# Gated scan: states between blocks of 128 tokens in place of two levels, blocks of 8 and pairs by one stationary tile, norm with tokens in partitions

## The chip, the cores and the metric

One core of a Trainium2 chip runs the whole program in one launch. The metric is the device time of an execution in microseconds (us). TensorE (PE; PEld is its weight load) multiplies, VectorE (DVE) and ScalarE (ACT) do the elementwise work, SyncE (SP) issues the loads.

## The reference, cut to what matters

A block (modulated norm, gated convolution, retention, MLP) is followed by a pooling mixer and a gated linear recurrence (HGRN2) with 16 heads of 128 channels over 512 tokens. The change lies in the recurrence alone:

```python
log_f = jnp.logaddexp(jnp.log(lbf), jnp.log1p(-lbf) + jax.nn.log_sigmoid(fz))
k = (1.0 - lbf) * jax.nn.sigmoid(-fz)
...
A = jnp.einsum('bhtd,bhsd,bhtsd->bhts', qc, kc, jnp.exp(diff))
o = jnp.einsum('bhts,bhsv->bhtv', A, vc) + jnp.einsum('bhtd,bhdv->bhtv', qc * jnp.exp(bc), S)
S = exp(b_last) * S + jnp.einsum('bhsd,bhsv->bhdv', kc * jnp.exp(b_last - bc), vc)
...
o = o * lax.rsqrt(jnp.mean(o * o, axis=-1, keepdims=True) + EPS)
return (o * norm_g * jax.nn.silu(gate)) @ w_out
```

So token t reads token s at or before it with the product of all forget gates f between them, channel by channel; each head's output is normed over its 128 channels and gated.

## The kernel before, in words

**Work and order.** Every large product is three TensorE matmuls in fp32r (weights and activations split in a high and a low part: `three`, L302 to L305; one such group of three over 512 tokens is called a triple here). The weights stream through SBUF in units of 128x1024: ScalarE makes the high part (L1405) and VectorE the low part (L704). In the scan, `project(h)` is three columns of eight triples for head h (forget gate, query, output gate: 24 triples, counted n = 0 to 23). The three engines run the same loop, each in its own program and its own strict order; semaphores tie them together. Between the triples, at the positions listed in `SIDE`, TensorE does one step of `mixing(h - 1)`, the attention of the head before; `norms` hands finished heads to a second side program (`turn`).

**Decay by levels.** VectorE's `prepare(h)` (n = 10 on) makes products of gates within blocks of 8 tokens around a pivot (`W`), their reciprocals (`IW`, L1262), and from them `f` and `qp`, whose product gives the scores inside each block of 8 (level 0, L586). Then the levels L = 8, 16, 32, 64, 128, 256: at each, the second half of a block of 2L tokens reads the first half. TensorE multiplies `k` by `q` (L597, L600, L604, L608); VectorE waits for that product, scales `q` and `k` in place by block totals to the next level (L1303, L1304), makes the next totals (L1309), and copies what it wants out of PSUM by mask (L1291, L1315) or ScalarE copies it (L1714 to L1726) into the score tile `A`, which covers 512x512 tokens. These products are plain f32 and each shows as two instructions.

**Output and norm.** Four matmuls with V stationary and rows of `A` moving (512, 384, 256 and 128 columns, L615) give the output with channels in partitions. ScalarE squares it, four matmuls with ones (L390) sum it over channels, VectorE gates it (L1323). Every fourth head VectorE takes the reciprocal root of all four heads' sums (`rsqrt`, L753 to L776, 13 small operations, each waiting for the one before), and for each head makes a diagonal tile (L784), TensorE spreads it by a product with ones (L412, in the next head's period), and VectorE multiplies (L1337).

Of the kernel before, what the change touches and what calls it, by code (L numbers as in the profile page):

```python
# [13 lines left out]
T = 512  # L14
# [114 lines left out]
def build(nc, a):  # L129
    with ExitStack() as ctx:  # L130
# [27 lines left out]
        PS = [ctx.enter_context(nc.psum_tensor(f"PS{i}", [128, T], F32)) for i in range(8)]  # L158
        with nc.sbuf_tensor("PSP", [128, 4, T], F32R) as PSP:
            pass  # L160
        QP0, QP1, W, IW = (sb(n, [128, T]) for n in ("QP0", "QP1", "W", "IW"))
        QP = [QP0, QP1]
# [15 lines left out]
        LVB, OB, RBK = [3, 4], 5, 6  # L178
        LEVELS = (8, 16, 32, 64, 128, 256)
        SIDE = (1, 3, 5, 8, 11, 14, 17, 19, 21, 23)  # L180
# [9 lines left out]
        class Head:  # L190


            def __init__(self, h):
                base = 4096 * (h % 2)
                self.A = hflat[:, base:base + 2048]
                self.diag = hflat[:, base:base + 2560].rearrange("p (i t) -> p i t", i=4)
                self.tot = hflat[:, base + 512:base + 640]
                self.q, self.f, self.k, self.sg = (
                    hflat[:, base + 2048 + T * i:base + 2560 + T * i] for i in range(4))
                self.qp = QP[h % 2][:, :]  # L200

            def totals(self, L):

                at = {8: 0, 16: 64, 32: 96, 64: 112, 128: 120}[L]
                return self.tot[:, at:at + T // L]
# [28 lines left out]
        gate = Count(sem("s_gate"))  # L234
        wfree, zfree = {}, {}
# [30 lines left out]
        def tensor_program(e):  # L266
# [306 lines left out]
            def mixing(h):  # L573
                t = Head(h)
                nl = 7 * h

                def level(L):
                    b = LVB[(nl + 1 + LEVELS.index(L) + 1) % 2] if L else LVB[(nl + 1) % 2]
                    claim(b)
                    return b, PS[b]  # L580

                b, ps = level(0)
                e.wait_ge(scaled.sem, scaled.of(h, 4))
                for i in range(4):
                    c = slice(128 * i, 128 * i + 128)
                    m = e.matmul(ps[:, c], t.f[:, c], t.qp[:, c], start=True, stop=True)  # L586
                m.then_inc(banks.full[b], banks.fill(("level", h, 0), b))
                yield
                for L in LEVELS:
                    b, ps = level(L)  # L590
                    k0, q1 = halves(t.k, L)[0], halves(t.q, L)[1]
                    e.wait_ge(scaled.sem, scaled.of(h, L))
                    if L <= 32:
                        for i in range(4):
                            c = slice(128 * i, 128 * i + 128)
                            o = ps[:, 64 * i:64 * i + 64].rearrange("p (n l) -> p n l", l=L)
                            m = e.matmul(o, t.k[:, c], halves(t.q[:, c], L)[1], start=True, stop=True)  # L597
                    elif L == 64:
                        for i in range(4):
                            m = e.matmul(ps[0:64, 64 * i:64 * i + 64], k0[:, i, :], q1[:, i, :],  # L600
                                         start=True, stop=True)
                    elif L == 128:
                        for i in range(2):
                            m = e.matmul(ps[:, 128 * i:128 * i + 128], k0[:, i, :], q1[:, i, :],  # L604
                                         start=True, stop=True)
                    else:
                        for i in range(2):
                            m = e.matmul(ps[:, 256 * i:256 * i + 256], t.k[:, 128 * i:128 * i + 128],  # L608
                                         t.q[:, 256:512], start=True, stop=True)
                    m.then_inc(banks.full[b], banks.fill(("level", h, L), b))  # L610
                    yield
                claim(OB)
                e.wait_ge(*banks.taken(("level", h, 256)))
                for i in range(4):
                    m = e.matmul(PS[OB][:, 128 * i:T], Z[:, h, 128 * i:128 * i + 128],  # L615
                                 t.A[:, 640 * i:512 * i + 512], start=i == 0, stop=i == 3)
                m.then_inc(banks.full[OB], banks.fill(("ho", h), OB))
                yield
                e.wait_ge(square.sem, square.of("ho", h))
                m = column_sums(TMP[:, 2 + h % 2, :], 4 * (h % 4), True, True)  # L620
                if h % 4 == 3:
                    m.then_inc(banks.full[7], banks.fill(("ho", "sums", h), 7))
                    norms.append(four_norms(h - 3))
                else:
                    m.then_inc(read.sem, read("ho", "sums", h))
                yield

            def four_norms(h):
                for i in range(4):
                    yield  # L630
                    spread(("ho norm", h + i), RBK)
                    yield
# [28 lines left out]
        def vector_program(e):  # L661
# [91 lines left out]
            def rsqrt(name, n, scale):  # L753

                x, y, t, xh = (NW[:, i, 0:n] for i in (4, 1, 2, 3))
                i0, i1 = NWI[:, 0, 0:n], NWI[:, 1, 0:n]
                e.wait_ge(*banks.made(name))
                e.tensor_scalar(x, PS[7][:, 0:n], scale, EPS, ALU.mult, ALU.add).then_inc(banks.free[7], 1)
                e.wait_ge(*banks.taken(name))
# [457 lines left out]
            e.memset(W[:, :], 1.0).then_inc(own.sem, own())  # L1217
# [17 lines left out]
            def prepare(h):  # L1235
                t, col = Head(h), slice(h, h + 1)
# [4 lines left out]
                yield  # L1241
                w8 = W[:, :].rearrange("p (n l) -> p n l", l=8)
                f8 = t.f.rearrange("p (n l) -> p n l", l=8)
                e.wait_ge(own.sem, own.of("f", h))
# [11 lines left out]
                e.tensor_tensor(t.tot[:, 64:128], w8[:, :, 0], f8[:, :, 0],  # L1256
                                ALU.mult).then_inc(own.sem, own("tl", h))
                for i in range(4):
                    yield
                    c = slice(128 * i, 128 * i + 128)  # L1260
# [3 lines left out]
                (q0, q1), (p0, p1), (w0, w1), (i0, i1), (k0, k1), (f0, f1) = (  # L1264
                    halves(x, 4) for x in (t.q, t.qp, W[:, :], IW[:, :], t.k, t.f))
# [21 lines left out]
            def mixing(h):  # L1287
# [38 lines left out]
                if h % 4 == 3:  # L1326
                    rsqrt(("ho", "sums", h), 16, 1.0 / 128)
                    norms.append(four_norms(h - 3))
# [571 lines left out]
```

## Time and profile before

| | us |
|---|---|
| median of 3 runs | 1631.62 |
| lowest, highest | 1627.57, 1631.91 |
| profiled execution | 1629.18 |
| its span, first to last instruction | 1627.4 |

A row of the timeline gives start, duration, engine, line, operation, tile written and read, shape, count, and in brackets the idle time of the engine before it. A matmul's duration includes its way through the array, so neighbours overlap: what one costs its engine is the distance from its start to the next start.

### The profile page before, as it was taken

How to read it: one execution, taken by the hardware profiler on the slowest of the kernel's cores; microseconds unless marked ns; L12 is line 12 of the kernel's file. 1: busy time of each engine (PE TensorE's matmuls, PEld its weight loads, DVE VectorE, ACT ScalarE, POOL GpSimd, SP SyncE). 2: the span in 40 equal slices, each digit the busy share in tenths (PEclk: the TensorE clock that was granted, in tenths of full speed). 3: DMA queues.
4: the chain of work that ended last, by engine and by line, in shares of the span. 5: the costliest groups of instructions: out<-in, count | busy, mean ns of one | idle time of the engine just before them, and what ended most of it. 6: DMA issues, size and time to landing. Idle time of an engine off the chain costs nothing.

```text
span 1627.4 us, 18077 instructions
## 1 busy us (share of the span) xinstructions
PE 1543.0 (95%) x7110; PEld 1259.5 (77%) x7110; DVE 978.5 (60%) x1740; ACT 468.7 (29%) x650; POOL 0.2 (0%) x4
## 2 busy tenths in 40 slices
PE   4899999499999999799999999999999999999996
PEld 4778778388888888578888788788888878878785
DVE  5985553754334333596568436328888797888534
ACT  1412122232323232342232225332222232222221
POOL 0000000000000000000000000000000000000000
PEclk9999999599999999899999999999999999999998
DMA  8645323034232323123323232321111211211211
GB/s 293 248 155 182 129 65 104 0 131 167 91 104 91 101 93 100 56 65 105 103 91 104 91 104 82 113 91 65 65 61 57 65 53 65 65 52 65 65 52 52
DMA packets 43891, 156.29 MB, mean 96 GB/s; under 512 B 4768, under 2 KB 5024, under 8 KB 43680
## 3 DMA queue, kind: packets, MB, share of 16 engines
q1 hardware_dynamic: 43808, 155.14, 28.3%
q8 instruction: 57, 0.93, 0.2%
q14 instruction: 26, 0.21, 0.0%
HBM read 153.03 MB, written 2.10 MB: 95 GB/s over the span
## 4 chain that ended last, share of the span: by engine, by line
PE 89%; DVE 8%; issue 1%; ACT 1%; DMA 1%; DVEq 0%; SPq 0%; ACTq 0%
PE PS L303 25%; PE PS L305 25%; PE PS L304 25%; PE PS L390 3%; PE PS L597 2%; PE PS L615 2%; PE PS L412 2%; PE PS L608 1%; PE PS L586 1%; PE PS L282 1%; DVE SQ L997 1%; PE PS L600 1%; DVE X L1020 1%; DVE Z L675 1%; DMA X<-in_x 1%
## 5 line engine op out<-in xcount | busy, mean ns | idle before, releaser
L303 PE MATMUL PS<-HH,WH 128*128 128x512 f32 x1152 | 484.1, 420 | 9.0 <-DVE HL L815 4.3
L305 PE MATMUL PS<-HH,WL 128*128 128x512 f32 x1152 | 453.0, 393 | 0.0
L304 PE MATMUL PS<-HL,WH 128*128 128x512 f32 x1152 | 451.5, 392 | 0.0
L704 DVE TENSOR_TENSOR WL<-RAW,WH 128x1024 fp32r<-128x1024 f32 x236 | 286.5, 1217 | 55.6 <-ACT WH L1405 53.4
L1405 ACT ACTIVATE WH<-RAW 128x1024 fp32r<-128x1024 f32 x236 | 248.0, 1052 | 224.5 <-PE PS L305 202.8
L303 PEld LDWEIGHTS PS<-HH,WH 128*128 128x128 f32 x1152 | 218.6, 190 | 61.3 <-issue 16.8
L304 PEld LDWEIGHTS PS<-HL,WH 128*128 128x128 f32 x1152 | 218.7, 190 | 48.3 <-issue 6.9
L305 PEld LDWEIGHTS PS<-HH,WL 128*128 128x128 f32 x1152 | 217.7, 189 | 48.4
L304 PE MATMUL PS<-ZL,WH 128*128 128x512 f32 x528 | 205.4, 389 | 0.0
L303 PE MATMUL PS<-ZH,WH 128*128 128x512 f32 x512 | 199.5, 390 | 1.6 <-issue 1.6
L305 PE MATMUL PS<-ZH,WL 128*128 128x512 f32 x512 | 199.2, 389 | 0.0
L733 DVE TENSOR_TENSOR ZL<-Z,ZH 128x512 fp32r<-128x512 f32 x64 | 43.9, 690 | 198.3 <-ACT ZH L1435 198.3
L304 PEld LDWEIGHTS PS<-ZL,WH 128*128 128x128 f32 x528 | 99.1, 188 | 20.7
L303 PEld LDWEIGHTS PS<-ZH,WH 128*128 128x128 f32 x512 | 96.1, 188 | 21.9 <-issue 1.9
L305 PEld LDWEIGHTS PS<-ZH,WL 128*128 128x128 f32 x512 | 96.1, 188 | 19.8
L1435 ACT ACTIVATE ZH<-Z 128x512 fp32r<-128x512 f32 x64 | 39.9, 630 | 209.8 <-PE PS L305 209.8
L1049 DVE TENSOR_TENSOR Z<-TMP 128x512 f32<-128x512 f32 x32 | 22.1, 692 | 100.1 <-ACT TMP L1592 100.0
L303 PE MATMUL PS<-WH,HH 128*128 128x512 f32 x160 | 63.7, 398 | 3.9 <-DVE HL L809 3.2
L304 PE MATMUL PS<-WL,HH 128*128 128x512 f32 x160 | 63.0, 394 | 0.0
L305 PE MATMUL PS<-WH,HL 128*128 128x512 f32 x160 | 62.9, 393 | 0.0
L390 PE MATMUL PS<-ONES,SQ 128*128 128x1 f32 x176 | 32.9, 316 | 28.9 <-ACT SQ L1472 11.6
L390 PEld LDWEIGHTS PS<-ONES,SQ 128*128 128x128 f32 x176 | 31.9, 280 | 33.7 <-DVE SQ L1027 11.9
(171 smaller groups left out, 1505.5 us busy)
## 6 DMA issues: line engine op xcount, KB each, us to landing
RAW<-in_w_fc SPq DMA_DIRECT2D x64, 512.0 KB, 3.3
RAW<-in_hgrn_in SPq DMA_DIRECT2D x64, 512.0 KB, 3.3
RAW<-in_ada SPq DMA_DIRECT2D x48, 512.0 KB, 3.8
RAW<-in_pool_in SPq DMA_DIRECT2D x40, 512.0 KB, 3.3
RAW<-in_w_in SPq DMA_DIRECT2D x28, 512.0 KB, 4.6
RAW<-in_pool_out SPq DMA_DIRECT2D x16, 512.0 KB, 3.3
RAW<-in_hgrn_out SPq DMA_DIRECT2D x16, 512.0 KB, 3.3
RAW<-in_w_out SPq DMA_DIRECT2D x8, 512.0 KB, 3.3
```

The lines of the kernel that those rows point to most:

```text
L303: e.matmul(out, wh, xh, start=first, stop=False)
L304: e.matmul(out, wh, xl, start=False, stop=False)
L305: return e.matmul(out, wl, xh, start=False, stop=last)
L390: m = e.matmul(PS[7][:, col + j:col + j + 1], src[:, 128 * j:128 * j + 128], ONES[:, 0:1], start=first and j == 0, stop=last, skip_group_c ...
L412: e.matmul(PS[b][:, :], ONES[:, :], DG[:, :], start=True, stop=True).then_inc(banks.full[b], banks.fill(name, b))
L597: m = e.matmul(o, t.k[:, c], halves(t.q[:, c], L)[1], start=True, stop=True)
L615: m = e.matmul(PS[OB][:, 128 * i:T], Z[:, h, 128 * i:128 * i + 128], t.A[:, 640 * i:512 * i + 512], start=i == 0, stop=i == 3)
L704: e.tensor_tensor(WL[:, s % NS, :], RAW[:, i % NR, :], WH[:, s % NS, :].bitcast(F32), ALU.subtract).then_inc(taken.sem, taken(i))
L733: e.tensor_tensor(ZL[:, z % NZ, :], Z[:, k, :], ZH[:, z % NZ, :].bitcast(F32), ALU.subtract).then_inc(zlo.sem, zlo(z))
L1049: e.tensor_tensor(Z[:, f, :], TMP[:, f % 2, :], TMP[:, f % 2, :], ALU.mult).then_inc(zdone.sem, zdone("fc1", f))
L1405: e.activation(WH[:, s % NS, :], RAW[:, i % NR, :], ACT.Copy).then_inc(whi.sem, whi(s))
L1435: e.activation(ZH[:, z % NZ, :], Z[:, k, :], ACT.Copy).then_inc(zhi.sem, zhi(z))
```

## The change

The blocks of 128 tokens are now tied by states and not by score levels.

- **Levels.** Levels 128 and 256 go. Level 0 and level 8 share one stationary tile: `f` of a block of 128 against `qp`, which is now 192 columns wide (128 tokens, and the 64 second-half tokens of the pairs scaled by `q8`). The product lies across two PSUM banks (`PAIR`). `q` and `k` go from the blocks of 8 straight to the scale of level 16 (`q8`, `q16`, `k16`). Level 32 is eight products with 32-column weights instead of four with 128.
- **States.** At the end of level 64, `k` of the first three blocks is transposed on TensorE ("kt"), ScalarE copies it (`KT`), three products with V ("ds") give what each block adds, and VectorE chains the states `ST` (a copy and two multiply-adds).
- **Output.** It has tokens in partitions: four products of 128 columns with the scores stationary and three with `q` against a state.
- **Norm.** ScalarE squares with a sum along the row (four operations), copies the output, and later scales by the root; `root` runs on 8 sums, every second head. TensorE transposes the result back (four transposes a head), and VectorE's last operation multiplies by the gain and the gate. The sums by ones, the diagonals and their products go.
- **Moved.** `f` and `k` are scaled by the lower bound on ScalarE instead of VectorE. Reciprocals leave out the pivot column of each block (32x3 twice, 32x4 twice). The positions in `SIDE` change.

The positions, then `mixing` and `two_norms` of `tensor_program`:

```diff
-        SIDE = (1, 3, 5, 8, 11, 14, 17, 19, 21, 23)
+        SIDE = (1, 3, 6, 9, 12, 15, 18, 20, 22, 23)
...
             def mixing(h):
+                e.wait_ge(scaled.sem, scaled.of(h, 8))
+                for i, c in enumerate(blocks):
+                    m = e.matmul(PAIR[:, 256 * i:256 * i + 192], t.f[:, c], t.qp[:, i, :], start=True, stop=True)
...
+                    m = e.matmul(PS[7][:, 64 * i:64 * i + 64].rearrange("p (n l) -> p n l", l=16), t.k[:, c],
+                                 halves(t.q[:, c], 16)[1], start=True, stop=True)
...
+                for i in range(8):
+                    m = e.matmul(PS[3][0:32, 32 * i:32 * i + 32], k0[:, i, :], q1[:, i, :], start=True, stop=True)
...
+                for c in blocks[0:3]:
+                    m = e.transpose(PS[7][:, c], t.k[:, c], IDN)
+                m.then_inc(banks.full[7], banks.fill(("kt", h), 7))
...
+                for c in blocks[0:3]:
+                    m = e.matmul(PS[3][:, c], KT[:, c], Z[:, h, c], start=True, stop=True)
...
+                for i, c in enumerate(blocks):
+                    m = e.matmul(PS[OB][:, c], t.diag[:, i, :], Z[:, h, c], start=i == 0, stop=i == 0,
+                                 skip_group_check=True)
+                e.wait_ge(*banks.taken(("ds", h)))
+                for i in range(1, 4):
+                    m = e.matmul(PS[OB][:, blocks[i]], t.q[:, blocks[i]], ST[:, blocks[i - 1]], start=False,
+                                 stop=True, skip_group_check=True)
...
+            def two_norms(h):
+                for i in range(2):
+                    yield
+                    claim(RBK)
+                    e.wait_ge(normed.sem, normed.of(h + i))
+                    for c in range(4):
+                        m = e.transpose(PS[RBK][:, 128 * c:128 * c + 128],
+                                        Z[:, h + i, 128 * c:128 * c + 128], IDN)
```

`prepare` and `mixing` of `vector_program`:

```diff
-                e.tensor_scalar(t.f, t.f, OMC[:, col], LBC[:, col], ALU.mult, ALU.add).then_inc(
-                    own.sem, own("f", h))
-                e.tensor_scalar(t.k, t.k, OMC[:, col], None, ALU.mult).then_inc(own.sem, own())
...
-                    e.reciprocal(IW[:, c], W[:, c]).then_inc(own.sem, own("iw", h, i))
+                    e.reciprocal(i8[:, n, l], w8[:, n, l]).then_inc(own.sem, own("iw", h, i))
...
+                e.tensor_tensor(t.q8, tl[:, :, 1], w7[:, :, 0], ALU.mult).then_inc(own.sem, own("q8", h))
+                e.tensor_tensor(t.q16, tl[:, :, 1], t8[:, :, 0], ALU.mult)
+                e.tensor_tensor(t.k16, w7[:, :, 0], t8[:, :, 1], ALU.mult)
...
+                e.tensor_tensor(t.qp[:, :, 128:192].rearrange("p i (n l) -> p i n l", l=8),
+                                p8[:, :, :, 1, :], by_pair(t.q8), ALU.mult).then_inc(scaled.sem, scaled(h, 8))
...
             def mixing(h):
+                e.wait_ge(*banks.made(("ds", h)))
+                e.tensor_copy(ST[:, 0:128], PS[3][:, 0:128]).then_inc(own.sem, own())
+                for i in (1, 2):
+                    e.wait_ge(own.sem, own.n)
+                    m = e.scalar_tensor_tensor(out=ST[:, 128 * i:128 * i + 128],
+                                               in0=ST[:, 128 * i - 128:128 * i], scalar=t.tot[128][:, i:i + 1],
+                                               in1=PS[3][:, 128 * i:128 * i + 128], op0=ALU.mult, op1=ALU.add)
...
+                if h % 2:
+                    e.wait_ge(*banks.taken(("ho", h)))
+                    e.tensor_scalar(NW[:, 4, 0:8], SSQ[:, 8 * (h // 2 % 2):8 * (h // 2 % 2) + 8], 1.0 / 128, EPS,
+                                    ALU.mult, ALU.add).then_inc(own.sem, own())
+                    e.wait_ge(own.sem, own.n)
+                    root(8)
```

`mixing` of `scalar_program`:

```diff
+                e.wait_ge(*banks.made(("kt", h)))
+                e.activation(KT, PS[7][:, 0:384], ACT.Copy).then_inc(banks.free[7], 1)
...
+                for c in range(4):
+                    i = 8 * (h // 2 % 2) + 4 * (h % 2) + c
+                    e.activation(TMP[:, 2 + h % 2, 128 * c:128 * c + 128], PS[OB][:, 128 * c:128 * c + 128],
+                                 ACT.Square, accum_out=SSQ[:, i:i + 1])
+                e.activation(Z[:, h, :], PS[OB][:, :], ACT.Copy).then_inc(banks.free[OB], 1)
```

## Rows read from the trace of the kernel before

**Rows 1.** The page: busy time of the engines, and the chain that ended last
```profile
PE 1543.0 (95%) x7110; PEld 1259.5 (77%) x7110; DVE 978.5 (60%) x1740; ACT 468.7 (29%) x650; POOL 0.2 (0%) x4
...
PE 89%; DVE 8%; issue 1%; ACT 1%; DMA 1%; DVEq 0%; SPq 0%; ACTq 0%
```

**Rows 2.** Windows: length, busy us and count of each engine, PEclk, DMA share, GB/s
```profile
1138.20:1243.50 105.30, 105.26 (x554) 85.57 (x553) 88.86 (x205) 28.86 (x49) 0.00 (x0) 1.00 0.19 61
```

**Rows 3.** Who TensorE waited for, 1108 to 1560 us: total, times, longest
```profile
PE PS L597 <- DVE Z L1304: 2.6, 2, 2.3
PE PS L303 <- DVE HL L1343: 1.3, 1, 1.3
```

**Rows 4.** The chain in order of time: start, us, what (first products of two heads)
```profile
1138.17 0.89 PE PS L586 x8
...
1243.47 0.89 PE PS L586 x8
```

**Rows 5.** Timeline of TensorE within one head's period
```profile
1163.39 1.05 PE L586 MATMUL PS<-QP,Z 128*128 128x128 f32 x8
1164.20 0.48 PE L303 MATMUL PS<-HH,WH 128*128 128x512 f32 x1
...
1164.98 0.39 PE L303 MATMUL PS<-HH,WH 128*128 128x512 f32 x1
...
1173.65 0.40 PE L305 MATMUL PS<-HH,WL 128*128 128x512 f32 x1
1173.97 0.68 PE L600 MATMUL PS<-Z 128*64 128x64 f32 x8
1174.58 0.50 PE L303 MATMUL PS<-HH,WH 128*128 128x512 f32 x1
...
1175.38 0.40 PE L303 MATMUL PS<-HH,WH 128*128 128x512 f32 x1
...
1179.30 1.02 PE L608 MATMUL PS<-Z 128*128 128x256 f32 x4
1179.97 0.58 PE L303 MATMUL PS<-HH,WH 128*128 128x512 f32 x1
...
1180.86 0.40 PE L303 MATMUL PS<-HH,WH 128*128 128x512 f32 x1
...
1186.70 0.40 PE L303 MATMUL PS<-HH,WH 128*128 128x512 f32 x1
...
1188.78 1.05 PE L586 MATMUL PS<-QP,Z 128*128 128x128 f32 x8
```

**Rows 6.** Timeline of TensorE's weight loads in the same head
```profile
1173.97 0.54 PEld L600 LDWEIGHTS PS<-Z 128*64 128x64 f32 x8 [0.36 <-issue]
```

**Rows 7.** Timeline of VectorE in the same head
```profile
1167.17 0.42 DVE L1304 TENSOR_TENSOR Z<-Z 128x256 f32<-128x256 f32 x1
1167.51 0.18 DVE L1309 TENSOR_TENSOR Z<-Z 128x32 f32<-128x32 f32 x1
1167.61 0.43 DVE L1315 COPY_PREDICATED Z<-MSK,PS 128x256 f32<-128x256 uint8 x1
...
1173.55 1.22 DVE L704 TENSOR_TENSOR WL<-RAW,WH 128x1024 fp32r<-128x1024 f32 x1
1174.68 0.28 DVE L1245 COPY W<-Z 128x128 f32<-128x128 f32 x1
...
1178.93 2.56 DVE L1262 RECIPROCAL IW<-W 128x128 f32<-128x128 f32 x3
```

**Rows 8.** Timeline of VectorE two heads later: first operation of the root, and what follows its last
```profile
1212.06 0.17 DVE L758 TENSOR_SCALAR NW<-PS 128x16 f32<-128x16 f32 x1
...
1214.45 0.68 DVE L1281 TENSOR_TENSOR Z<-Z,W 128x512 f32<-128x512 f32 x1
```

**Rows 9.** Groups by line and shape, 1060 to 1627 us: count, busy, mean ns, idle before
```profile
L586 PE MATMUL PS<-QP,Z 128*128 128x128 f32 x128 | 16.9, 275 | 0.1
...
L1715 ACT ACTIVATE Z<-PS 32x128 f32<-32x128 f32 x16 | 4.3, 270 | 0.2
```

More of the change, by code:

```diff
@@ L234, in build @@
         gate = Count(sem("s_gate"))
+        normed = Count(sem("s_normed"))
         wfree, zfree = {}, {}
@@ L574, in mixing @@
                 t = Head(h)
[L575 to L583, printed above, removed]
+                blocks = [slice(128 * i, 128 * i + 128) for i in range(4)]
+                claim(3)
+                claim(4)
+                e.wait_ge(scaled.sem, scaled.of(h, 8))
@@ new lines, in mixing @@
+                m.then_inc(banks.full[7], banks.fill(("level", h, 16), 7))
+                yield
+                claim(3)
+                e.wait_ge(scaled.sem, scaled.of(h, 32))
+                k0, q1 = halves(t.k, 32)[0], halves(t.q, 32)[1]
+                for i in range(8):
+                    m = e.matmul(PS[3][0:32, 32 * i:32 * i + 32], k0[:, i, :], q1[:, i, :], start=True, stop=True)
+                m.then_inc(banks.full[3], banks.fill(("level", h, 32), 3))
+                yield
+                claim(4)
@@ L584, in mixing @@
+                e.wait_ge(scaled.sem, scaled.of(h, 64))
+                k0, q1 = halves(t.k, 64)[0], halves(t.q, 64)[1]
                 for i in range(4):
-                    c = slice(128 * i, 128 * i + 128)
-                    m = e.matmul(ps[:, c], t.f[:, c], t.qp[:, c], start=True, stop=True)
-                m.then_inc(banks.full[b], banks.fill(("level", h, 0), b))
+                    m = e.matmul(PS[4][0:64, 64 * i:64 * i + 64], k0[:, i, :], q1[:, i, :], start=True, stop=True)
+                m.then_inc(banks.full[4], banks.fill(("level", h, 64), 4))
@@ L588, in mixing @@
                 yield
[L589 to L611, printed above, removed]
@@ L612, in mixing @@
-                claim(OB)
[L613 to L616, printed above, removed]
+                claim(7)
+                e.wait_ge(scaled.sem, scaled.of(h, 128))
+                for c in blocks[0:3]:
+                    m = e.transpose(PS[7][:, c], t.k[:, c], IDN)
+                m.then_inc(banks.full[7], banks.fill(("kt", h), 7))
@@ L621, in mixing @@
[L621 to L625, printed above, removed]
+                if h % 2:
+                    norms.append(two_norms(h - 1))
                 yield
-            def four_norms(h):
-                for i in range(4):
+            def two_norms(h):
+                for i in range(2):
                     yield
-                    spread(("ho norm", h + i), RBK)
+                    claim(RBK)
[3 more added lines that the diff above has]
+                                        Z[:, h + i, 128 * c:128 * c + 128], IDN)
+                    m.then_inc(banks.full[RBK], banks.fill(("ho norm", h + i), RBK))
@@ L1325, in mixing @@
                 yield
[L1326 to L1333 removed]
+                e.wait_ge(own.sem, own.of("tot", h, 128))
+                e.wait_ge(*banks.made(("ds", h)))
+                e.tensor_copy(ST[:, 0:128], PS[3][:, 0:128]).then_inc(own.sem, own())
@@ L1755, in scalar_program @@
                         next(side, None)
+                        next(turn, None)
                     if n == 0 and h:
                         side = mixing(h - 1)
+                        turn = norms.pop() if norms else turn
                 run(side)
-            for f in range(3, 7):
-                run(column())
-            z_first(8, normed)
+            turn = norms.pop()
+            for f in range(3, 6):
+                for n, _ in enumerate(column()):
+                    if n % 2:
+                        next(turn, None)
+            run(turn)
+            run(column())
+            z_first(8, gated)
             run(column())
@@ L1766, in scan_out @@
                 pair_square("hout", n, f)
-            rows(16, LATE, normed, scan_out, 8)
+            rows(16, LATE, gated, scan_out, 8)
         for program in (tensor_program, vector_program, scalar_program):
@@ L1773, in build @@
         for c in (read, taken, zlo, hlo, tdone, plow, diag, zdone, scaled, sums, own, whi, zhi, hhi, phigh,
-                  square, copied, gate, banks):
+                  square, copied, gate, normed, banks):
             c.settle()
```

265 lines of the change are left out of this document (152 added, 113 removed).

## The prediction

> **What bounds the kernel now.** I read the page first. TensorE is busy for 1543.0 of 1627.4 us, and 89% of the chain that ended last is TensorE's [rows 1]. Next the windows of the scan: in a stretch of 105.30 us that holds four heads TensorE is busy for 105.26 and VectorE for 88.86, and the granted clock is 1.00, the 2.4 GHz level [rows 2]. The waits agree: from 1108 to 1560 us TensorE waited on another engine three times, 3.9 us in all [rows 3]. So a head costs what TensorE's queue costs. From the first product of one head to that of the head four later are 1243.47 - 1138.17 = 105.30 us [rows 4], 26.33 a head, the norm's four spreading products included; a head without them takes 1188.78 - 1163.39 = 25.39 [rows 5].
>
> The three projection columns are not changed. Three triples between 1186.70 and 1188.78 take 2.08, so one takes 0.693, and 24 take 16.63. **The products of the scan itself and of the norm then cost 26.33 - 16.63 = 9.70 us a head now.** This is what the change rebuilds.
>
> **Prices on TensorE.** Eight f32 instructions with 128 columns (four products) start at 1163.39 and the next triple at 1164.20: 0.81, or 0.101 each. The triple behind them takes 0.78 instead of 0.693, so a group costs 0.09 more [rows 5]. Four with 256 columns take 0.67, and the triple behind them 0.89: 0.87 in all, 0.22 each. An instruction with 192 columns lies between 0.11 and 0.22; I take 0.165. Eight with 64-column weights (L600) start 0.09 after the end of the triple before them (1173.65 + 0.23), take 0.61 (0.076 each) and lengthen the next triple by 0.11: 0.81.
>
> **The new sum for a head.**
> - Level 0 with level 8: 8 x 0.165 = 1.32.
> - Level 16, as before, 8 instructions: 0.90. Level 64, unchanged: 0.81.
> - Level 32: 16 instructions with 32-column weights, which no row shows. 128 columns cost 0.101 and 64 cost 0.076; the same line gives 0.064 at 32, so 16 x 0.064 + 0.20 = 1.22. Bounds: half of 0.076 gives 0.81, no gain from narrowness 16 x 0.101 + 0.20 = 1.82.
> - The states: six instructions, 6 x 0.101 + 0.09 = 0.70. The output: 14 instructions, 1.50.
> - Transposes, three for the states and four for the norm: no row shows one. Bounds: two instructions each, as for any f32 product here, 0.70 and 0.90; or one each, 0.39 and 0.49. I take one: the second instruction carries the rest of an f32 product's mantissa, and fp32r products show in the same rows as one instruction each; a transpose sums nothing.
>
> That is 7.33 us with single transposes, 8.05 with double ones. The saving is 2.37 or 1.65 a head, 37.9 or 26.4 us over 16.
>
> On level 32 the Trainium skill (TensorE: Matmul & The Clock Gate, LDWEIGHTS) would go further: it puts a load at its columns over 1.2 GHz, 27 ns for 32, so the group would cost 0.63 and 9 us more would be saved. The rows agree at 128 columns (107 against 101 ns) and not at 64 (53 against 76), so I stay with the line.
>
> A duration is not a price: the 128-column product has a mean of 275 ns [rows 9] and costs 101. The same page (Part 4: PE-mode transpose) gives a transpose about 275 ns in one kernel's context and so speaks for the dearest of the rivals below, while its section Terms says that the transpose mode is 4 times faster for FP32, which speaks for one pass. No run so far shows either.
>
> **VectorE, which must keep ahead.** It has 88.86 busy of 105.30 [rows 2], and the change takes more from it than it adds: two scalings go to ScalarE, one level's scaling, the diagonals and the spread's multiply go; small products, three state operations and a root every two heads come. What counts is its order. In `prepare` the pair product `scaled(h, 8)` releases the next head's first group on TensorE. Both engines start from level 64 (n = 9), where VectorE waits for the product. TensorE then has 0.81, 16 triples (11.09), the transposes 0.39, states 0.70, output 1.50: **14.49 us**. VectorE has: the product's landing 1.0; scalings of 256 columns at 0.34 and a total at 0.10 (starts 1167.17, 1167.51, 1167.61 [rows 7]), 0.78; copy 0.2, low part of weights 1.13 (1173.55 to 1174.68), two chained products of 128 columns 0.4 each, two of 64 columns 0.2 each, 2.53; reciprocals, 0.85 for 128 columns (2.56 for three), 3.5 such, 2.98; query copy 0.6; state chain 0.95; five operations of 256 columns 1.70; `t8` 0.2; weights again 1.13; four small ones 0.4; landing 0.1. That is **12.4 us**, a margin of 2.1. The state chain stands ahead of half a reciprocal run there, and waits for "ds"; the last two reciprocals and all that follow queue behind it. That is in the sum.
>
> In every second head the root is put between these steps (n = 20). Before, it took 1214.45 - 1212.06 = 2.39 [rows 8]; with one more chained step some 2.6. That is 0.5 more than the margin: TensorE waits 0.5 us at level 0 in every second head, 4.0 in all. With double transposes the margin is 0.31 more, 1.6 in all.
>
> **ScalarE.** It has 28.86 of 105.30 [rows 2]. Per head it gains two scalings of 512 columns, the copy of the transposes, three more operations for the squares, a copy, four for the norm: far from full. Its squares lie ahead of the root. 128 columns take 0.27 [rows 9]; what the sum along the row adds is shown nowhere, between nothing and doubling the four (1.1). Part of it meets VectorE's lead; I take 0.4 us a pair, 3.2 in all, bounds 0 and 6.4. The scalings moved there (0.6 before `f` is ready) fall while VectorE is still in its level 64 step; if that cover went, they would add to the 12.4. Nothing changes in SP's and POOL's queues: no load is added or moved.
>
> The end of the scan: now two heads are normed after the last one instead of four, which is in the sum; the waits on `HL` and L1304 there [rows 3] I leave as they are. Memory clears before the scan get shorter, under TensorE's projection: nothing.
>
> **Sum:** 37.9 - 4.0 - 3.2 = 30.7. The profiled execution took 1629.18 us, so 1598.5; the median shown is 2.4 above it, so **1601 us** as a median.
>
> **Rivals.**
> - *Dear transposes.* Two instructions each: 26.4 - 1.6 - 3.2 = 21.6, 1610. For it: every f32 product here shows twice. Against: nothing is summed. Or one each that doesn't overlap and pays a duration of 275 ns [rows 9]: 7 x 0.275 = 1.93 instead of 0.88, 17 us of the saving go, 1618; against it, 275 ns products run 101 ns apart.
> - *Hand-overs come late.* At levels 16 to 64 TensorE has two or three triples (1.4 to 2.1) for landing 0.2 and two scalings with their landing, 0.8: 0.4 to 1.1 spare. If VectorE, behind the weights' low part and the gate (1.13 + 0.6), misses five of them by 0.3, 24 us go: 30.7 - 24 = 6.7, 1625. Against: laid out from the same rows, its previous step ends before the product does.
> - *Slower: narrow weights don't overlap.* Before the first L600 the weight load stood idle for 0.36 [rows 6]. If each of the 16 loads of level 32 waits so, the group costs 5.8 instead of 1.22, 4.5 x 16 = 73 more: 1674. It decides from (1.22 + 30.7/16)/16 = 0.20 us an instruction on. Against: inside L600 the distance is 0.076.
> - *The change gives nothing*, since its gain returns as waits of several small kinds: 1631.
>
> **How the numbers follow.** Forecast 0.53, dear transposes 0.25, late hand-overs 0.11, slower 0.07, nothing 0.04. A measurement tells some 0.3%, 4.9 us, from no change. Faster: 0.53 + 0.25 + most of the late case, 0.88; same 0.04; slower 0.08. Low end: no waits (7.2) and level 32 at 0.81 (6.6) give 1587; high end: double transposes with level 32 at 1.82 (9.6) 1620. Range 1589 to 1620; outside it lie the slow case, nothing, half of the late one and the far tails, near 2 in 10.
>
> **What would show it.** Right: two heads take about 48.5 us instead of 52.65; seven transposes a head show one instruction each, some 0.1 us apart; level 32 takes about 1.2; the only regular wait of TensorE is on the pair product, every second head, about 0.5 us; the clock stays at 1.00. Wrong: transposes shown twice; TensorE idle ahead of levels 32 or 64 or of the output; level 32 over 3 us.

## The result, and the profile after

The changed kernel takes a median of 1590.6 us (4 runs, 1587.45 to 1591.84) against 1630.66 for the kernel before (4 runs, 1627.57 to 1631.91). The ratio is 0.9754 with an interval of 0.9733 to 0.9775: 40.1 us less. The prediction had 30.7 less and 1601 (1.0 of the difference in the medians is the kernel before, which it had at 1631.62). The profiled execution took 1591.84, with a span of 1590.1.

The page of the kernel after, busy times and the chain that ended last, answering to [rows 1]:

```profile
PE 1502.0 (94%) x7126; PEld 1233.2 (78%) x7126; DVE 947.3 (60%) x1761; ACT 516.3 (32%) x858; POOL 0.2 (0%) x4
...
PE 82%; DVE 14%; issue 2%; ACT 1%; DMA 1%; DVEq 0%; SPq 0%; ACTq 0%
```

TensorE is still the bound: its busy time fell by 1543.0 - 1502.0 = 41.0 us, VectorE's by 31.2, and ScalarE took on 47.6. VectorE's share of the chain rises from 8% to 14%: every second head TensorE now stands waiting for it a moment, and the chain then follows VectorE's work back.

Window of the scan after, six pairs of heads (columns as in [rows 2]):

```profile
1161.86:1445.78 283.92, 281.71 (x1668) 234.56 (x1669) 244.91 (x631) 122.55 (x300) 0.00 (x0) 1.00 0.20 68
```

The ends of this window are the starts of a head's first product, from the chain of the kernel after in order of time, as in [rows 4]:

```profile
1161.86 1.54 PE PS L585 x8
...
1256.51 1.54 PE PS L585 x8
...
1445.78 1.54 PE PS L585 x8
```

A pair of heads takes 283.92 / 6 = 47.32 us where it took 105.30 / 2 = 52.65. That is 5.33 less, 42.6 for eight pairs. The whole run got 40.1 of it. The granted clock is 1.00, the 2.4 GHz level, in both. Of the 47.32 us TensorE is idle for (283.92 - 281.71) / 6 = 0.37, and who it waited for is in the waits of TensorE from 1118 to 1470 us (total, times, longest), as in [rows 3]:

```profile
PE PS L585 <- DVE QP L1314: 2.6, 7, 0.4
PE PS L307 <- DVE HL L1396: 0.6, 1, 0.6
```

One wait for each pair of heads, on the pair product, of 0.35 to 0.4 us of idle time. The prices of the parts stand in the timeline of TensorE within two heads, answering to [rows 5]:

```profile
1209.18 1.54 PE L585 MATMUL PS<-QP,Z 128*128 128x192 f32 x8 [0.35 <-DVE QP L1314]
...
1212.77 0.61 PE L646 MATMUL PS<-CST,Z 128*128 128x128 f32 x4
1213.14 0.47 PE L307 MATMUL PS<-HH,WH 128*128 128x512 f32 x1
...
1228.08 0.48 PE L307 MATMUL PS<-HH,WH 128*128 128x512 f32 x1
...
1232.98 1.47 PE L585 MATMUL PS<-QP,Z 128*128 128x192 f32 x8
1234.15 0.53 PE L307 MATMUL PS<-HH,WH 128*128 128x512 f32 x1
...
1234.98 0.39 PE L307 MATMUL PS<-HH,WH 128*128 128x512 f32 x1
...
1237.95 0.40 PE L307 MATMUL PS<-HH,WH 128*128 128x512 f32 x1
...
1238.74 0.69 PE L601 MATMUL PS<-Z 128*32 128x32 f32 x16
1239.36 0.50 PE L307 MATMUL PS<-HH,WH 128*128 128x512 f32 x1
...
1240.18 0.40 PE L307 MATMUL PS<-HH,WH 128*128 128x512 f32 x1
...
1241.66 0.68 PE L608 MATMUL PS<-Z 128*64 128x64 f32 x8
...
1244.44 0.49 PE L615 MATMUL PS<-CST,Z 128*128 128x128 f32 x3
1244.69 0.48 PE L307 MATMUL PS<-HH,WH 128*128 128x512 f32 x1
...
1245.47 0.39 PE L307 MATMUL PS<-HH,WH 128*128 128x512 f32 x1
...
1249.60 1.05 PE L627 MATMUL PS<-Z 128*128 128x128 f32 x8
1250.49 0.83 PE L631 MATMUL PS<-Z 128*128 128x128 f32 x6
1251.08 0.48 PE L307 MATMUL PS<-HH,WH 128*128 128x512 f32 x1
```

Read each group as the prediction did: from its start to the triple behind it, plus what that triple takes beyond 0.693. Level 32 (L601) shows how: the triple ahead should have ended at 1237.95 + 0.69 = 1238.64, so 0.10 is lost before it; 0.62 to the next triple; that one takes 1240.18 - 1239.36 = 0.82, which is 0.12 too long. 0.84 in all. The same for each group:

| group, us a head | predicted | measured |
|---|---|---|
| level 0 with level 8 (L585) | 1.32 | 1.17 + 0.14 = 1.31 |
| level 16 (L593) | 0.90 | 0.90 |
| level 32 (L601) | 1.22 | 0.84 |
| level 64 (L608) | 0.81 | 0.81 |
| transposes for the states (L615, three) | 0.39 | 0.25 + 0.09 = 0.34 |
| what each block adds (L621) | 0.70 | 0.58 + 0.09 = 0.67 |
| output (L627, L631) | 1.50 | 1.48 + 0.09 = 1.57 |
| norm's transposes (L646, four) | 0.49 | 0.40 (0.37 to 0.42) |
| sum | 7.33 | 6.84 |

Twice 16.63 + 6.84 is 46.94, and the period less the 0.60 that the wait costs (below) is 46.72. So this sum is 0.11 a head too dear: triples away from a group take a little less than 0.693 (the seven behind the output 4.90 with 0.09 of the group's edge in it, 0.687 each). That each transpose is one instruction is in the counts: 4 of L646 and 3 of L615 a head.

VectorE's side of the wait, in its timeline behind level 64 of a head with the root, answering to [rows 8]:

```profile
1253.62 0.18 DVE L1376 TENSOR_SCALAR NW<-SSQ 128x8 f32<-128x8 f32 x1
...
1255.95 0.42 DVE L1314 TENSOR_TENSOR QP<-QP,Z 128x256 f32<-128x256 f32 x1
```

Both engines start from level 64 at 1241.66. The pair product ends at 1255.95 + 0.42 = 1256.37, and TensorE begins the next head 0.14 later, at 1256.51. So VectorE's way, landing included, is 14.85 us, of which the root is 1255.95 - 1253.62 = 2.33 and the rest 12.52. What that costs TensorE stands in the starts. The seven triples between the output and the next head take 1232.98 - 1228.08 = 4.90 us in a head without the root and 1256.51 - 1251.08 = 5.43 in a head with it: TensorE starts 0.53 late. Level 0 behind the wait then takes 1210.42 - 1209.18 = 1.24 to the next triple instead of 1.17, so a pair loses 0.60. The wait view has only 0.37 of it, since it counts from the end of the last matmul, whose duration (0.39) runs on for 0.16 after the next one could start (0.23). TensorE's own way over the same steps is 14.85 - 0.53 = 14.32. VectorE's margin without the root is 14.32 - 12.52 = 1.80, and the root of 2.33 overruns it by the 0.53.

ScalarE's timeline in the same head, the sums along the row ahead of that root:

```profile
1251.36 0.28 ACT L1782 ACTIVATE TMP<-PS 128x128 f32<-128x128 f32 x1 [5.90 <-PE PS L631]
1251.53 0.19 ACT L1782 ACTIVATION_READ_ACCUMULATOR TMP<-PS 128x1 f32 x1
1251.62 0.27 ACT L1782 ACTIVATE TMP<-PS 128x128 f32<-128x128 f32 x1
...
1252.28 0.22 ACT L1782 ACTIVATION_READ_ACCUMULATOR TMP<-PS 128x1 f32 x1
```

Each square with its sum takes 0.26 from start to start, and the last sum is over at 1252.28 + 0.22 = 1252.50, 1.1 us before the root begins.

### The profile page after: what moved, and what is told of

The parts are those of the page before. It is cut to its first block, busy times and chain, and to the rows that moved or that the text cites. A ratio compares the mean times of both kernels' runs of the same rounds, so it can differ in the third digit from the quotient of the medians.

```text
span 1590.1 us, 18291 instructions
## 1 busy us (share of the span) xinstructions
PE 1502.0 (94%) x7126; PEld 1233.2 (78%) x7126; DVE 947.3 (60%) x1761; ACT 516.3 (32%) x858; POOL 0.2 (0%) x4
## 4 chain that ended last, share of the span: by engine, by line
PE 82%; DVE 14%; issue 2%; ACT 1%; DMA 1%; DVEq 0%; SPq 0%; ACTq 0%
PE PS L307 24%; PE PS L309 24%; PE PS L308 24%; PE PS L394 2%; DVE WL L721 2%; PE PS L585 1%; DVE DG L1279 1%; PE PS L416 1%; PE PS L593 1%; PE PS L286 1%; PE PS L601 1%; PE PS L608 1%; DVE SQ L1018 1%; DVE X L1041 1%; DVE Z L692 1%
## 5 line engine op out<-in xcount | busy, mean ns | idle before, releaser
L307 PE MATMUL PS<-HH,WH 128*128 128x512 f32 x1152 | 476.7, 414 | 9.3 <-DVE HL L836 4.3
L394 PE MATMUL PS<-ONES,SQ 128*128 128x1 f32 x176 | 33.7, 321 | 29.0 <-ACT SQ L1525 11.6
```

Of the source, the lines that this page charges most:

```text
L307: e.matmul(out, wh, xh, start=first, stop=False)
L394: m = e.matmul(PS[7][:, col + j:col + j + 1], src[:, 128 * j:128 * j + 128], ONES[:, 0:1], start=first and j == 0, stop=last, skip_group_c ...
```

## The experiments

The period of two heads is read in each run as above, from the chain of first products (or of level 16) over six pairs, in e8 over five. "Before" is the kernel before on the same chip; the runs are from several chips, and these medians of before lie within 0.9 us of each other.

| run | median us (before) | ratio, interval | two heads, us |
|---|---|---|---|
| the change | 1590.6 (1630.66) | 0.9754, 0.9733 to 0.9775 | 47.32 |
| e1, products for transposes | 1601.55 (1629.77) | 0.9824, 0.9807 to 0.984 | 48.98 |
| e2, wide weights at level 32 | 1592.88 (1629.77) | 0.977, 0.975 to 0.979 | 47.49 |
| e3, pair's tile not shared | 1597.62 (1629.77) | 0.9803, 0.9787 to 0.9818 | 48.30 |
| e6, levels for states | 1602.2 (1629.77) | 0.9832, 0.9817 to 0.9846 | 48.69 |
| e7, norm alone | 1608.4 (1630.28) | 0.9865, 0.9844 to 0.9886 | 49.78 |
| e4, root later | 1586.65 (1630.08) | 0.9735, 0.9721 to 0.9748 | 46.90 |
| e5, scalings on VectorE | 1595.11 (1630.08) | 0.9785, 0.977 to 0.98 | 48.26 |
| e8, e4 with e5 | 1592.97 (1630.28) | 0.9766, 0.9747 to 0.9784 | 47.84 |

**e1: are the transposes really one pass?** The seven transposes of a head become plain f32 products with the identity, at the same places.

```diff
-                    m = e.transpose(PS[7][:, c], t.k[:, c], IDN)
+                    m = e.matmul(PS[7][:, c], t.k[:, c], IDN, start=True, stop=True)
...
-                        m = e.transpose(PS[RBK][:, 128 * c:128 * c + 128],
-                                        Z[:, h + i, 128 * c:128 * c + 128], IDN)
+                        m = e.matmul(PS[RBK][:, 128 * c:128 * c + 128],
+                                     Z[:, h + i, 128 * c:128 * c + 128], IDN, start=True, stop=True)
```

> The seven transposes a head become plain f32 products with the identity (the same numbers, but two instructions each). Theory (TensorE's queue sets the pace and a transpose is one pass): 7 x 0.101 = 0.71 us a head more, less up to 0.3 a pair that the wait at level 0 shrinks by; two heads take 48.4 to 48.7 instead of 47.3, the whole run is 9 to 11 us longer than the changed kernel. Rival (a transpose pays like an f32 product already, or its duration of about 275 ns): no change, within 2 us.

Timeline of TensorE in this run, the transposes for the states:

```profile
1196.91 0.83 PE L615 MATMUL PS<-CST,Z 128*128 128x128 f32 x6
1197.50 0.48 PE L307 MATMUL PS<-HH,WH 128*128 128x512 f32 x1
```

Six instructions stand where three stood, and take 0.59 to the next triple instead of 0.25. Two heads take 1.66 more, for 14 more instructions: 0.12 each, a little over the 0.101 of a product's instruction. The run is 11 us longer. So the transposes of the change are single, and the rival of dear transposes fell at this point. 48.98 is above the 48.4 to 48.7 expected: an added instruction cost 0.12 and not 0.101, and the wait on the pair product did not shrink (2.5 over 7 times), since VectorE's way from level 64 grew along with TensorE's, from 14.85 to 15.15 (1243.14 to 1258.29).

**e2: does the narrowness of level 32 gain or lose?** Four products with 128-column weights in place of eight with 32, ScalarE copying the diagonal pieces.

```diff
-                for i in range(8):
-                    m = e.matmul(PS[3][0:32, 32 * i:32 * i + 32], k0[:, i, :], q1[:, i, :], start=True, stop=True)
+                for i, c in enumerate(blocks):
+                    m = e.matmul(PS[3][:, 64 * i:64 * i + 64].rearrange("p (n l) -> p n l", l=32), t.k[:, c],
+                                 halves(t.q[:, c], 32)[1], start=True, stop=True)
```

> Level 32 again as four products with 128-column weights (8 instructions) instead of eight with 32-column weights (16 instructions). By the prices read from the changed kernel (0.84 a head with narrow weights, 0.90 with wide ones): 0.06 a head, 1 us longer in all, hardly to be told. By the line of the prediction (narrow 1.22): 5 us shorter. By loads that don't overlap: shorter by more than 5 us.

Timeline of TensorE in this run at level 32:

```profile
1212.77 1.00 PE L600 MATMUL PS<-Z 128*128 128x64 f32 x8
1213.57 0.48 PE L307 MATMUL PS<-HH,WH 128*128 128x512 f32 x1
```

0.80 to the next triple instead of 0.62, and two heads are only 0.17 longer (the wait, 3.1 over 7, is 0.07 of that). Narrow weights neither cost what the slower rival feared nor bring anything worth the name: with the 0.2 at its edges the group of 16 narrow instructions takes 0.84, with 0.09 the group of 8 wide ones 0.90.

**e3: what does sharing one stationary tile save?** The 192-column product is split, 128 columns and 64, with the same `f`.

```diff
-                    m = e.matmul(PAIR[:, 256 * i:256 * i + 192], t.f[:, c], t.qp[:, i, :], start=True, stop=True)
+                    e.matmul(PAIR[:, 256 * i:256 * i + 128], t.f[:, c], t.qp[:, i, 0:128], start=True, stop=True)
+                    m = e.matmul(PAIR[:, 256 * i + 128:256 * i + 192], t.f[:, c], t.qp[:, i, 128:192],
+                                 start=True, stop=True)
```

> Level 0 and level 8 as two products with the same stationary tile (128 and 64 columns) instead of one with 192: 16 instructions instead of 8. Theory (instruction count and not columns is the price below 128 columns): 1.31 becomes about 1.8, 0.49 a head, two heads 48.3, 8 us longer in all. Rival (columns are the price, or the tile that is already loaded is not loaded again): no change, within 2 us.

Window of six pairs in this run (columns as above):

```profile
1163.56:1453.36 289.80, 287.59 (x1766) 240.42 (x1766) 245.47 (x631) 122.62 (x301) 0.00 (x0) 1.00 0.20 66
```

48.30 a pair, 0.98 more, which is 0.49 a head as priced (1.79 as two groups against 1.31). The weight loads grew by 97 and the matmuls by 98 over the same 12 heads: the second product loads the same tile again. What is saved is instructions, and an instruction of 192 columns is cheaper than one of 128 with one of 64.

**e6: what do the states save?** Levels 128 and 256 come back with ten output products, and the norm and output stay with tokens in partitions. Core of the edit:

```diff
-                    m = e.transpose(PS[7][:, c], t.k[:, c], IDN)
...
-                    m = e.matmul(PS[3][:, c], KT[:, c], Z[:, h, c], start=True, stop=True)
...
+                    m = e.matmul(PS[7][:, 128 * i:128 * i + 128], t.k[:, blocks[2 * i]], t.q[:, blocks[2 * i + 1]],
+                                 start=True, stop=True)
...
+                    m = e.matmul(PS[3][:, 256 * i:256 * i + 256], t.k[:, blocks[i]], t.q[:, 256:512],
+                                 start=True, stop=True)
...
+                for a, (i, j) in enumerate(((0, 1), (2, 3), (0, 2), (0, 3), (1, 2), (1, 3))):
+                    m = e.matmul(PS[OB][:, blocks[j]], FAR[:, 128 * a:128 * a + 128], Z[:, h, blocks[i]],
+                                 start=False, stop=True, skip_group_check=True)
```

> Levels 128 and 256 come back in place of transposes, states and their chain; output with tokens in partitions and the new norm stay (ten products for the output instead of seven). Theory (TensorE's queue): 0.45 + 0.87 + 20 instructions 2.11 = 3.43 instead of 0.34 + 0.67 + 1.57 = 2.58, 0.85 a head, two heads 48.7 to 49.0, 11 to 14 us longer in all; the wait at level 0 may go, since the state chain no longer stands in VectorE's order. Rival (the gain came from the norm alone): no change, within 2 us.

Window of six pairs in this run:

```profile
1162.71:1454.82 292.11, 292.11 (x1730) 245.18 (x1729) 242.58 (x619) 129.31 (x312) 0.00 (x0) 1.00 0.20 66
```

TensorE never waits here: busy equals length. Two heads take 48.69, against 281.71 / 6 = 46.95 of busy TensorE in the change: 0.87 a head of TensorE work, as the prices have it (level 128 0.45, level 256 0.86 and output 2.16, together 3.47, against 0.34 + 0.67 + 1.57 = 2.58). But 0.36 of the 1.74 a pair comes back as the wait on VectorE. The run is 11.6 us longer than the change, so the rival, that the norm alone made the gain, fell.

**e7: the norm alone.** e6 with the edits of e2 and e3 as well, so that of TensorE's products only the norm's and the output's orientation differ from before.

```diff
-                    m = e.matmul(PAIR[:, 256 * i:256 * i + 192], t.f[:, c], t.qp[:, i, :], start=True, stop=True)
+                    e.matmul(PAIR[:, 256 * i:256 * i + 128], t.f[:, c], t.qp[:, i, 0:128], start=True, stop=True)
...
-                for i in range(8):
+                for i, c in enumerate(blocks):
...
-                    m = e.transpose(PS[7][:, c], t.k[:, c], IDN)
+                    m = e.matmul(PS[7][:, 128 * i:128 * i + 128], t.k[:, blocks[2 * i]], t.q[:, blocks[2 * i + 1]],
+                                 start=True, stop=True)
```

> Only the new norm and its output with tokens in partitions are left of what TensorE gains: levels 128 and 256 are back, level 0 and level 8 are two products again, level 32 has its 128-column weights again. Theory (the parts add, on TensorE's queue): the pair tile 0.98 and the narrow weights 0.15 on top of the levels' run, 48.69 + 1.13 = 49.8 for two heads; against the kernel before (52.65) 2.8 a pair or 23 us in all, so the norm would be over half of the change. Rival (the parts overlap, the norm alone gives most of it): two heads under 49 us, the run as fast as that with the levels alone.

Window of six pairs in this run:

```profile
1164.67:1463.37 298.70, 298.70 (x1731) 255.39 (x1730) 242.32 (x619) 129.31 (x313) 0.00 (x0) 1.00 0.19 64
```

49.78 a pair, and 2.87 under the 52.65 of before. The steps then add up: from before to the norm alone 2.87, to e6 (shared tile and narrow level 32) another 1.09, to the change (states) 1.37: 5.33. **The norm is more than half of the gain** (21.9 of about 40 us on the clock). The prices say the same: before, a head's four sums by ones took 0.90 (1185.11 to 1185.91, and 0.10 on the next triple) and its spreading product 0.94 (26.33 - 25.39); four transposes take 0.40. That is 1.44 less a head, 2.88 a pair.

**e4: is the wait the root's place?** The root comes one step later in VectorE's order, behind the pair product.

```diff
                 yield
                 yield
+                yield
                 if h % 2:
                     e.wait_ge(*banks.taken(("ho", h)))
```

> VectorE takes the root of every second head two positions later (n = 22 instead of 20), behind the pair product that releases the next head's first group on TensorE. Theory (the root is what makes TensorE wait 0.35 us in every second head): that wait goes, two heads take 46.9 to 47.0 instead of 47.3, 2.5 to 3 us less in all. Rival (the lateness is only handed on): TensorE waits as long at level 16 or for the norm's transposes, no change.

Waits of TensorE in this run from 1118 to 1470 us, and the window of six pairs:

```profile
PE PS L307 <- DVE HL L1397: 1.8, 2, 1.2
```
```profile
1158.23:1439.62 281.39, 281.24 (x1670) 235.51 (x1669) 244.89 (x631) 122.72 (x300) 0.00 (x0) 1.00 0.21 68
```

Timeline of TensorE in this run, level 16 of a head and the norm's transposes:

```profile
1207.60 1.00 PE L593 MATMUL PS<-Z 128*128 128x64 f32 x8
1208.64 0.63 PE L646 MATMUL PS<-CST,Z 128*128 128x128 f32 x4
```

The wait on the pair product is gone (the two waits left are around the last head), a pair takes 46.90, 0.42 less. So the root's place is the cause of that wait. The rival was right for a part: the norm's transposes, which want the root, now start 1.04 behind level 16 instead of 1212.77 - 1211.94 = 0.83. Of the 0.60 won, about 0.2 a pair is handed on to them, and the wait view does not list it. This version is ahead of both kernels in its median, 1586.65; its interval against before overlaps that of the change, and the two were not timed on one chip together, so the 4 us between them rest on the period more than on the clock: eight times 0.42 is 3.4.

**e5: does the move of the scalings to ScalarE matter?** `f` and `k` are scaled on VectorE again, ahead of everything that leads to the pair product.

```diff
-                e.activation(t.f, t.f, ACT.Identity, scale=OMC[:, h:h + 1], bias=LBC[:, h:h + 1]).then_inc(
-                    gate.sem, gate("f", h))
-                e.activation(t.k, t.k, ACT.Copy, scale=OMC[:, h:h + 1]).then_inc(gate.sem, gate("k", h))
...
+                e.tensor_scalar(t.f, t.f, OMC[:, h:h + 1], LBC[:, h:h + 1], ALU.mult, ALU.add).then_inc(
+                    own.sem, own("f", h))
+                e.tensor_scalar(t.k, t.k, OMC[:, h:h + 1], None, ALU.mult).then_inc(own.sem, own())
```

> The two scalings of f and k by the lower bound go back from ScalarE to VectorE, as before the change: 0.86 us of issue more per head in front of the pair product. Theory (what counts is VectorE's order up to the pair product, margin 2.1 without the root and -0.35 with it): in heads with the root the wait grows from 0.35 to about 1.2, in the others there is still margin; two heads take about 48.2, 6 to 7 us more in all. Rival (VectorE is idle for 6.5 of 47.3 us a pair and takes it up): no change, within 2 us.

Waits of TensorE in this run from 1118 to 1470 us, then TensorE and VectorE at the output of a head:

```profile
PE PS L585 <- DVE QP L1318: 7.8, 7, 1.1
```
```profile
1227.67 1.05 PE L627 MATMUL PS<-Z 128*128 128x128 f32 x8
...
1227.86 0.73 DVE L1370 SCALAR_TENSOR_TENSOR Z<-Z,PS 128x128 f32<-128x128 f32 x2
...
1228.64 0.94 PE L631 MATMUL PS<-Z 128*128 128x128 f32 x6
```

The wait grows from 0.37 to 1.1 in the heads with the root, and the others still have none on the pair product: their margin takes it. Of the 0.94 that a pair is longer, 0.74 is that wait. Another 0.18 is a second late hand-over, at the output of the head behind it: the products with the states (L631) start 0.97 behind the first products where 0.89 is normal, and take 0.69 instead of 0.59 to the next triple. They wait for VectorE's state chain, which ends at 1227.86 + 0.73 = 1228.59; the wait view counts this as busy TensorE. On the clock it is 4.5 us.

**e8: with the root later, is there room for the scalings?** Both edits of e4 and e5 together.

```diff
+                yield
                 if h % 2:
...
+                e.tensor_scalar(t.f, t.f, OMC[:, h:h + 1], LBC[:, h:h + 1], ALU.mult, ALU.add).then_inc(
+                    own.sem, own("f", h))
...
```

> The late root together with the two scalings back on VectorE. Theory (VectorE's order against TensorE's, head by head): in the run with the late root the scaling to level 16 ends 0.5 us before its product starts in heads with the root; 0.86 more makes that product 0.3 to 0.4 us late, two heads take 47.2 to 47.3, some 3 us more than with the late root alone. Rival (with the root out of the way VectorE has margin for both): two heads take 46.9, no wait at level 16.

Waits of TensorE in this run from 1118 to 1470 us, then VectorE, ScalarE and TensorE in its timeline behind the root:

```profile
PE PS L593 <- DVE Z L1328: 2.7, 7, 0.4
```
```profile
1256.43 0.69 DVE L1158 TENSOR_TENSOR TMP<-PS,RB 128x512 f32<-128x512 f32 x1
...
1257.21 0.63 ACT L1754 ACTIVATE Z<-TMP 128x512 f32<-128x512 f32 x1 [4.49 <-DVE TMP L1158]
...
1257.75 1.26 ACT L1795 ACTIVATE Z<-Z,NW 128x128 f32<-128x128 f32 x4
...
1257.93 1.08 PE L593 MATMUL PS<-Z 128*128 128x64 f32 x8 [0.38 <-DVE Z L1328]
...
1259.15 0.63 PE L646 MATMUL PS<-CST,Z 128*128 128x128 f32 x4
```

The wait came back at level 16, as forecast; in starts it is 0.54 us (two triples ahead of it take 2.05, 1255.88 to 1257.93, and 1.51 in e4). The period, 47.84, is 0.94 over that of e4 and longer than forecast, because two other things came late. The output's products with the states lose 0.18, as in e5. And the norm's transposes start 1259.15 - 1257.93 = 1.22 behind level 16, where e4 has 1.04 and the change 0.83. They want ScalarE's four scalings by the root (L1795, at an end of 1259.01), these queue behind the sigmoid of the gate (L1754), and that waits for VectorE's gate sum (L1158) behind the root. The wait view lists neither, the distances of the starts do.

## Why the prediction was right, and where not

**The bound and the sum's method held.** TensorE's queue set the time before and after, so the gain is what the scan's products cost less, minus the waits: 5.33 us a pair, 42.6 in all. The clock shows 40.1. What is missing lies at the end of the scan, as the timeline of TensorE and a window of the kernel after show:

```profile
1480.75 0.67 PE L601 MATMUL PS<-Z 128*32 128x32 f32 x16 [2.71 <-DVE Z L1347]
1481.35 0.53 PE L307 MATMUL PS<-HH,WH 128*128 128x512 f32 x1
...
1485.19 0.68 PE L608 MATMUL PS<-Z 128*64 128x64 f32 x8
```
```profile
1481.68:1485.09 3.41, 3.41 (x9) 2.33 (x7) 0.67 (x3) 0.36 (x2) 0.00 (x0) 0.50 0.08 30
```

Around the last head TensorE waits for 0.56, 1.21 and 2.71 us, 4.5 in all, where the kernel before waits for 1.30 and 2.28 (the other 0.34 of [rows 3] is in the first head). Behind the last of these waits the granted clock is 0.50, the 1.2 GHz level, for 3.41 us. Three triples take 1485.19 - 1481.35 = 3.84 there, and 2.30 at the same place of a head in the middle (1239.36 to 1241.66). So in this execution 1.5 us went to the clock and 0.9 to longer waits, 2.4 of the 2.5. The kernel before keeps 1.00 there (1495 to 1520 us), and so do e1 and e7 (1480 to 1505 us); the six other runs show the fall too. It is 1.5 of the 2.3 us by which e1's 11 us on the clock fall short of 8 x 1.66 = 13.3. The prediction left the waits at the scan's end as they were and gave the clock no term.

The two profiled spans differ by 37.3 only, because the scan itself starts 2.9 us later in the one after (last matmul ahead of it at 1114.36, before at 1111.44). That is not the change: e2, e3, e4 and e7, the same up to there, start it at 1111.1 to 1111.7.

**The 9.4 us by which it was off** come from these terms, all but one on the careful side:
- *Level 32* is the step that failed in size. "The same line gives 0.064 at 32", and so 1.22, was a line through two points; it measured 0.84: 16 instructions with 0.039 us from start to start, and 0.22 once for the group. That is 0.38 x 16 = 6.1 us. The lower bound of 0.81 was the right neighbour. On this the Trainium skill (TensorE: Matmul & The Clock Gate, LDWEIGHTS) gives a load as its columns over 1.2 GHz, 27 ns for 32: by that an estimate of 0.63 for the group. The run stands between that and the line, nearer to the Trainium skill's figure.
- *The other groups*: 0.11 a head too dear together, 1.8 us; the transposes most, which cost 0.34 and 0.40, not 0.39 and 0.49. The triples away from a group, 0.687 and not 0.693, are another 0.11 a head, 1.8 us.
- *ScalarE's 3.2* do not exist. "Part of it meets VectorE's lead" was wrong at both ends: the sum along the row adds nothing to the distance of 0.26 (two copies of 128 columns without a sum start 0.26 apart before, at 1172.34 and 1172.60), and the squares are over 1.1 us before the root.
- *The root's wait* costs 0.60 a pair, 4.8 us and not 4.0. Its mechanism was right: one wait, in every second head, at level 0, and e4 takes it away by moving the root alone. Its size, 0.53 late for 0.5, came near because errors cancelled: TensorE's way was 14.32 for 14.49, VectorE's 12.52 for 12.4, and the root 2.33 for 2.6 (13 operations as before, where it took 2.39, and no chained step on top). The 0.07 that the late group loses was in no term.

6.1 + 1.8 + 1.8 + 3.2 - 0.8 = 12.1, less the 2.5 at the scan's end: 9.6, which is the 9.4 within rounding.

**Luck.** 1590.6 lies 1.6 us above the low end of the range. The 2.4 us that the scan's end lost, which the prediction did not foresee, are what kept it inside: without them it is 1588.2, under the 1589. And "about 48.5 us" for two heads did not follow from the prediction's own sum, which gives 52.65 - 30.7 / 8 = 48.8; 47.32 was measured.

**The transposes** were the main doubt, and the choice bore out: one instruction each, some 0.1 us, and e1 shows what two would have cost, 11 us. The reason given (nothing is summed, so no second instruction) is not shown: in e1 the product with the identity gives the same numbers and takes two. That double transposes would ease the wait by 0.31 failed too, since e1 has the same wait. The Trainium skill (TensorE: Matmul & The Clock Gate, Terms) has the transpose mode 4 times faster for FP32; the counts agree that it is the cheaper one, with half the instructions. The 275 ns that the Trainium skill gives on that page for a bf16 transpose in one kernel's context (Part 4: PE-mode transpose) agree with the mean duration of L646 and L615 (279 and 272, below), and not with what they cost.

Groups by line and shape of the kernel after, 1060 to 1590 us (columns as in [rows 9]):

```profile
L646 PE MATMUL PS<-CST,Z 128*128 128x128 f32 x64 | 10.0, 279 | 0.0
L615 PE MATMUL PS<-CST,Z 128*128 128x128 f32 x48 | 7.8, 272 | 0.0
```

**The other rivals.** Late hand-overs at levels 16 to 64 did not happen: no such wait in six pairs, and one of 2.71 at level 32 in the last head. The slower case, narrow weights that wait for each load, failed as its own "against" had it: the 0.36 of idle weight load [rows 6] comes once before a group and not before each load. It shows with 32 columns too, in the weight loads of the kernel after:

```profile
1238.74 0.58 PEld L601 LDWEIGHTS PS<-Z 128*32 128x32 f32 x16 [0.36 <-issue]
```

**VectorE's cover.** That the moved scalings "would add to the 12.4" if they stayed is what e5 shows: 0.74 more wait in each root head.

**What stayed open**: why the clock falls at the scan's end after and not before, where TensorE waits there too; how many of the executions without a profile have the fall; and why a transpose takes one instruction.

## What to carry to other kernels

When one engine's queue is full, price every group by the distance from its start to the next start, add what the neighbour loses, and sum: here that came within 0.6 us of 24 a head, where mean durations (275 ns for an instruction that costs 101) would have given nearly three times the price. Read a wait from the starts as well: the idle time showed 0.37 of 0.60, and late hand-overs in e4, e5 and e8 stand in no wait view. In a strict queue, put long chains of small operations behind the one result that the full engine waits for next; this moved 0.42 us a pair for one line. Before giving work back to an engine that shows 14% of idle time, look at the hand-overs that it feeds: e5 lost 0.9 us a pair against the change, and e8 as much against e4, on an engine that was idle for a seventh of the window.

## What the runs showed of the hardware

- With 32-column weights and 32 moving columns, f32 instructions start 0.039 us apart (16 in 0.62), with 64 0.076, with 128 0.101; a group pays some 0.2 once at its edges with narrow weights, and 0.09 with 128 columns. With their edges, eight wide ones (0.90) and sixteen narrow ones (0.84) come nearly to the same.
- An f32 transpose of 128x128 on TensorE is one instruction, an f32 product two.
- Two f32 products in a row with the same stationary tile load it twice (e3).
- On ScalarE a sum along the row shows as an instruction of its own (0.19 to 0.22 us), but overlaps: 0.26 from square to square, against a duration of 0.27 for one 128-column operation.
- In the last head of the kernel after, behind waits of 0.56, 1.21 and 2.71 us within 13 us, TensorE's granted clock was 0.50 for 3.41 us; three triples took 3.84 us there instead of 2.30.
